# Row sums of a gathered expert layer: both dot products of a pair first, its weights and sums in the same place

## The chip, the cores and the metric

The kernel runs on one core of one Trainium2 chip. The metric is device time of one launch in microseconds (us). The engines are TensorE (PE in the rows, PEld for its weight loads), VectorE (DVE), ScalarE (ACT), GpSimd (POOL) and SyncE (SP); 16 DMA engines move data.

## The reference

A two-block model on 256 tokens of width 1024, all in float32. The part that the change touches is the expert layer of the first block (`peer_ffn`). It runs three times: on the context tokens in layer 0, on the x tokens in layer 0, on the x tokens in layer 1.

```python
def block(args):            # one block of 128 tokens
    hk, ek, gk = args       # tokens [128, 1024], chosen experts [128, 128], gates [128, 128]
    act = jax.nn.gelu(jnp.einsum('ted,td->te', u[ek], hk), approximate=False)
    return jnp.einsum('te,ted->td', gk * act, v[ek])
```

Each token chooses 128 of 16384 experts (8 heads, 16 each, from sums of scores). For each chosen expert a vector u is dotted with the token, the result goes through gelu, is multiplied by the gate and weighs a vector v; the 128 weighted v are summed. Everything else (modulation, a gated recurrence, convolutions, attention, a Fourier convolution, two MLPs) surrounds this.

## The kernel before, in words

The 128 tokens of a tile lie on the 128 partitions. A "row" below is one choice n of all 128 tokens: one indirect DMA from GpSimd (line 2652) gathers 128 pieces of 8 KB, the u and the v of the expert that each token chose, 1 MB in all, into one of `SLOTS` = 6 slots of the buffer `uv`. There are 3 x 2 x 128 = 768 rows, in the order of the list `SELS`, which has seven segments (`SEGS`, line 368): 128 rows of the context tile 0, 32 of context tile 1, 128 + 128 of x in layer 0 (segments 2 and 3, "the x stretch"), the remaining 96 of context tile 1, and 128 + 128 of x in layer 1.

What is done with row j:

- `dot(j)` on VectorE (line 2351): multiply the u half by the token tile (`hA` or `hB`) and add up into a column of `dots`. It shows as CUSTOM_DVE_ANT_0 followed by a small DVE_READ_ACCUMULATOR2_ANT.
- gelu on ScalarE (line 1616), one instruction for both rows of a pair, `dots` to `coef`.
- `weigh(j)` on VectorE: for a row that `on_pe(j)` names, a 128x128 diagonal matrix with coef times gate, written over the head of the slot (line 2361, TENSOR_SCALAR); for any other, coef times gate in one column (line 2363).
- the row sum: for a row on PE two matmuls of the diagonal with the v half, 512 columns each, added up in two PSUM banks (line 1137; each shows as two matmul records because of float32); otherwise one SCALAR_TENSOR_TENSOR on VectorE into `acc` (line 2375; the first of a segment is line 2372). After the last row of a segment `flush` adds both sums to the tokens.

The gather of row j waits until row j - 6 is summed (lines 2640 to 2644), in order of j. A row's slot is therefore taken from the gather's issue until its sum.

`weave` (line 571) sets the order on each engine. It goes over pairs of rows g = 0 to 255 (first weave, ahead of the last layer's mixer) and 256 to 383 (second weave). At each g it issues `segment(g)` and then those pieces of other streams that are due at g by hand-written numbers: projections, recurrence, the choice of experts, modulations, filters. Each engine has its own `segment` and its own pieces of the same numbers, so the instruction order on each engine is fixed. VectorE's `segment(g)` (line 2402) issues: dot of row 2g, weights of the pair g - 1, the VectorE sum of row 2g - 2 if it has one, dot of row 2g + 1, the VectorE sum of row 2g - 1 if it has one. TensorE's `segment(g)` (line 1141) issues the matmuls of the rows of pair g - 1. ScalarE's (line 1611) issues the gelu of pair g.

`on_pe` (line 378): in the x stretch three rows of four are summed on PE (j % 4 != 0), elsewhere every odd row, and in the last 64 rows none.

The weights of all other work come through a ring of two slots of 2 MB, loaded by SyncE's queue as TensorE frees them.

Of the kernel before, what the change touches and what calls it, by code (L numbers as in the profile page):

```python
# [16 lines left out]
ACT = mybir.ActivationFunctionType  # L17
# [54 lines left out]
def program(nc, A, out):  # L72
# [14 lines left out]
    with ctx:  # L87
# [98 lines left out]
        dot_done = sem("dot_done")  # L186
        gelu_done = sem("gelu_done")
# [185 lines left out]
        SEG_END = list(itertools.accumulate(hi - lo for _, _, lo, hi in SEGS))  # L373
# [3 lines left out]

        def on_pe(j):
            w, t, n, seg = SELS[j]
            if seg in (2, 3):  # L380
                return j % 4 != 0
            return j % 2 == 1 and (seg < 6 or n < NSEL // 2)

        pe_upto = list(itertools.accumulate((on_pe(j) for j in range(len(SELS))), initial=0))
# [88 lines left out]
        dots = a.take(4)  # L473
        coef = a.take(4)
# [881 lines left out]
        def _(act):  # L1356
# [254 lines left out]
            def segment(g, first, last):  # L1611

                if g < last:
                    c = slice((g % 2) * 2, (g % 2 + 1) * 2)
                    act.wait_ge(dot_done, 2 * (g + 1))
                    act.activation(coef[:, c], dots[:, c], ACT.Gelu).then_inc(gelu_done, 1)  # L1616

            def kv_pieces():
                for c, dst in enumerate((kcN[:, :, 0:CW], kcN[:, :, CW:D], vN[:, 0:NT, 0:CW], vN[:, 0:NT, CW:D])):
# [162 lines left out]
            for c in range(6):  # L1782
                chunk_there(L_hin, c)
                e = L_hin.e0 + c
                for b in range(4):
                    j = 4 * c + b
# [18 lines left out]
        def _(dve):  # L1805
# [548 lines left out]
            def weigh(j):  # L2354

                p, t, n, seg = SELS[j]
                c = coef[:, column(j):column(j) + 1]
                gate = gates[:, p % 2, t, n:n + 1]
                dve.wait_ge(gelu_done, j // 2 + 1)
                if on_pe(j):  # L2360
                    dve.tensor_scalar(uv[:, j % SLOTS, 0:P], ident[:, :], c, gate, ALU.mult, ALU.mult).then_inc(diag_ready, 1)  # L2361
                else:
                    dve.tensor_tensor(c, c, gate, ALU.mult).then_inc(coef_ready, 1)
# [37 lines left out]

            def segment(g, first, last):

                done = (2 * g - 2, 2 * g - 1) if g > first else ()
                for s in range(2):
                    if g < last:
                        dot(2 * g + s)
                    if s == 0:
                        for j in done:
                            weigh(j)  # L2410
                    if done and not on_pe(done[s]):
                        add_row(done[s])
                if done and 2 * g in SEG_END:
                    flush(SEG_END.index(2 * g))

            def early_mods():
                for c in range(10, 12):
# [334 lines left out]
```

## Time and profile before

| | |
|---|---|
| median of 3 runs | 4079.06 us (4070.0 to 4091.91) |
| the profiled execution | 4078.86 us, span 4077.1 us |
| mean granted TensorE clock | 0.845 of full |
| PE busy | 2923.2 us (72%) |
| DVE busy | 2702.6 us (66%) |
| ACT busy | 669.4 us (16%) |
| POOL busy | 935.1 us (23%) |
| DMA, gathers (queue q0) | 812.33 MB, 51.6% of 16 engines' span |
| DMA, weights and rest (queue q1) | 336.37 MB, 22.8% |

The first row's dot starts at 302.6 us and the last row's at 3186.9 us; between about 2196 and 2344 us the gathers pause for the last layer's mixer. Busy time is not a limit by itself: a stretch ends when its last wait ends. In the rows, "idle before <-releaser" names what ended an engine's idle time.

### The profile page before, as it was taken

How to read it: one execution, taken by the hardware profiler on the slowest of the kernel's cores; microseconds unless marked ns; L12 is line 12 of the kernel's file. 1: busy time of each engine (PE TensorE's matmuls, PEld its weight loads, DVE VectorE, ACT ScalarE, POOL GpSimd, SP SyncE). 2: the span in 40 equal slices, each digit the busy share in tenths (PEclk: the TensorE clock that was granted, in tenths of full speed). 3: DMA queues.
4: the chain of work that ended last, by engine and by line, in shares of the span. 5: the costliest groups of instructions: out<-in, count | busy, mean ns of one | idle time of the engine just before them, and what ended most of it. 6: DMA issues, size and time to landing. Idle time of an engine off the chain costs nothing.

```text
span 4077.1 us, 31583 instructions
## 1 busy us (share of the span) xinstructions
PE 2923.2 (72%) x10786; PEld 1692.8 (42%) x10786; DVE 2702.6 (66%) x5411; ACT 669.4 (16%) x1113; POOL 935.1 (23%) x794
## 2 busy tenths in 40 slices
PE   7988698757888765567976676674570475978598
PEld 2956376324322122224743443111130353967396
DVE  2657968786767678466687577678878754445454
ACT  1311101000000001101002110000000242523053
POOL 0002223333323233233231033233344100000000
PEclk9999799778999887788987878886685697988799
DMA  6359899899999987988996399999899522544144
GB/s 247 123 181 371 301 350 361 330 365 343 368 393 400 368 323 283 345 325 324 356 376 227 124 347 359 384 387 348 334 391 369 203 89 68 186 173 157 57 163 147
DMA packets 277096, 1156.42 MB, mean 284 GB/s; under 512 B 19128, under 2 KB 19769, under 8 KB 178201
## 3 DMA queue, kind: packets, MB, share of 16 engines
q0 software_dynamic: 112768, 812.33, 51.6%
q1 hardware_dynamic: 162584, 336.37, 22.8%
q10 hardware_dynamic: 1600, 5.96, 0.4%
q8 instruction: 71, 1.16, 0.1%
q14 instruction: 73, 0.59, 0.0%
HBM read 1150.46 MB, written 4.13 MB: 283 GB/s over the span
## 4 chain that ended last, share of the span: by engine, by line
PE 40%; DMA 27%; DVE 23%; issue 8%; ACT 1%; POOL 0%; SPq 0%; POOLq 0%; DVEq 0%; PEldq 0%
DMA arena<-in_peer_uv,arena 17%; PE ps L1137 7%; DMA ring<-in_w_mod 7%; PE ps L747 5%; PE ps L749 5%; PE ps L748 5%; PE ps L866 4%; DVE arena L2351 4%; PE ps L1054 3%; DVE arena L2375 3%; PE ps L977 2%; PE ps L732 1%; PE ps L852 1%; DVE w_lo L1927 1%; DVE arena L2361 1%
## 5 line engine op out<-in xcount | busy, mean ns | idle before, releaser
L1137 PE MATMUL ps<-arena 128*128 128x512 f32 x1664 | 1017.2, 752 | 610.1 <-DVE arena L2361 609.8
L2652 POOL DMA_INDIRECT arena<-in_peer_uv,arena x768 | 921.2, 1200 | 2253.1 <-PE ps L1137 846.9
L1137 PEld LDWEIGHTS ps<-arena 128*128 128x128 f32 x1664 | 359.0, 232 | 1196.4 <-DVE arena L2361 801.1
L2351 DVE CUSTOM_DVE_ANT_0 arena<-arena,hA 128x1024 f32<-128x1024 f32 x512 | 624.9, 1223 | 294.2 <-DMA arena<-in_peer_uv,arena 289.3
L2351 DVE CUSTOM_DVE_ANT_0 arena<-arena,hB 128x1024 f32<-128x1024 f32 x256 | 312.8, 1222 | 265.8 <-DMA arena<-in_peer_uv,arena 264.5
L1616 ACT ACTIVATE arena<-arena 128x2 f32<-128x2 f32 x384 | 78.2, 204 | 2384.9 <-DVE arena L2351 2384.3
L2375 DVE SCALAR_TENSOR_TENSOR arena<-arena 128x1024 f32<-128x1024 f32 x345 | 441.0, 1278 | 0.1
L1927 DVE TENSOR_TENSOR w_lo<-ring,w_hi 128x1024 fp32r<-128x1024 f32 x220 | 264.2, 1223 | 161.5 <-ACT w_hi L1396 154.2
L866 PE MATMUL ps<-ring,condS 128*2 128x512 f32 x576 | 284.6, 641 | 77.2 <-DMA ring<-in_w_mod 77.2
L747 PE MATMUL ps<-hT_hi,w_hi 128*128 128x256 f32 x992 | 287.5, 290 | 25.4 <-DVE hT_lo L1935 24.8
L749 PE MATMUL ps<-hT_hi,w_lo 128*128 128x256 f32 x992 | 284.5, 287 | 0.0
L748 PE MATMUL ps<-hT_lo,w_hi 128*128 128x256 f32 x992 | 283.2, 286 | 0.0
L1396 ACT ACTIVATE w_hi<-ring 128x1024 fp32r<-128x1024 f32 x220 | 231.3, 1060 | 239.5 <-DMA ring<-in_w_mlp_out 90.3
L747 PEld LDWEIGHTS ps<-hT_hi,w_hi 128*128 128x128 f32 x992 | 193.2, 195 | 27.7 <-issue 26.8
L1054 PE MATMUL ps<-hT,ring 128*128 128x256 f32 x896 | 201.1, 380 | 1.6 <-ACT hT L1426 1.6
L798 PE MATMUL ps<-ident,hA 128*128 128x128 f32 x128 | 25.5, 376 | 239.5 <-DVE hA L1977 198.5
L748 PEld LDWEIGHTS ps<-hT_lo,w_hi 128*128 128x128 f32 x992 | 193.1, 195 | 0.0
L749 PEld LDWEIGHTS ps<-hT_hi,w_lo 128*128 128x128 f32 x992 | 192.3, 194 | 0.0
L1054 PEld LDWEIGHTS ps<-hT,ring 128*128 128x128 f32 x896 | 170.9, 191 | 44.2 <-issue 21.1
L866 PEld LDWEIGHTS ps<-ring,condS 128*2 128x2 f32 x576 | 45.2, 88 | 307.2 <-issue 217.0
L1101 PE MATMUL ps<-hT,ring 128*128 128x256 f32 x640 | 146.6, 384 | 0.0
L1101 PEld LDWEIGHTS ps<-hT,ring 128*128 128x128 f32 x640 | 124.4, 195 | 33.2 <-issue 17.9
(314 smaller groups left out, 3440.6 us busy)
## 6 DMA issues: line engine op xcount, KB each, us to landing
ring<-in_w_mod SPq DMA_DIRECT2D x48, 2048.0 KB, 19.9
ring<-in_w_in SPq DMA_DIRECT2D x16, 2048.0 KB, 15.3
ring<-in_w_mlp_in SPq DMA_DIRECT2D x64, 512.0 KB, 6.1
ring<-in_w_mlp_out SPq DMA_DIRECT2D x64, 512.0 KB, 5.7
ring<-in_peer_wq SPq DMA_DIRECT2D x12, 2048.0 KB, 16.3
ring<-in_w_in SPq DMA_DIRECT2D x44, 512.0 KB, 5.9
vec<-mods SPq DMA_DIRECT2D x27, 512.0 KB, 8.1
ring<-in_w_out SPq DMA_DIRECT2D x6, 2048.0 KB, 9.0
```

The costliest lines, as they stand in the source:

```text
L747: pe.matmul(out_, stationary[0], moving[0], start=first, stop=False)
L748: pe.matmul(out_, stationary[0], moving[1], start=False, stop=False)
L749: return pe.matmul(out_, stationary[1], moving[0], start=False, stop=last)
L866: mm = pe.matmul(o, condS[:, k, 2 * (l // 2):2 * (l // 2) + 2], ring[:, s, k, :], start=k == 0, stop=k == KT - 1)
L1054: mm = pe.matmul(o, ring[:, s, k, b * P:(b + 1) * P], hT[:, k, :], start=k == 0, stop=k == KT - 1)
L1101: mm = pe.matmul(o, ring[:, s, k, b * P:(b + 1) * P], hT[:, k, :], start=k == 0, stop=k == KT - 1)
L1137: mm = pe.matmul(ps[:, 6 + c, :], uv[:, j % SLOTS, 0:P], uv[:, j % SLOTS, D + c * CW:D + (c + 1) * CW], start=start, stop=stop)
L1396: act.activation(w_hi[:, s, ks, :], ring[:, s, ks, :], ACT.Copy).then_inc(high_done, 1)
L1927: dve.tensor_tensor(w_lo[:, s, ks, :], ring[:, s, ks, :], w_hi[:, s, ks, :].bitcast(F32), ALU.subtract).then_inc(low_done, 1)
L2351: dve.tensor_tensor_reduce(row, row, peer_buf[p][:, t, :], 1.0, 0.0, ALU.mult, ALU.add, dots[:, column(j):column(j) + 1]).then_inc(dot_don ...
L2375: ins = dve.scalar_tensor_tensor(acc, row, c, acc, ALU.mult, ALU.add)
L2652: pool.indirect_dma_start(uv[:, j % SLOTS, :], None, A["peer_uv"], at).then_inc(uv_full[j % SLOTS], 16)
```

## The change

Three edits. VectorE's `segment(g)` issues both dots of pair g, then (after a flush, if a segment of rows ended) the weights of the same pair g and its VectorE sums; before, weights and sums were those of the pair g - 1. ScalarE's gelu is one instruction for each row, with its own wait and its own signal, and `weigh(j)` waits for the gelu of row j alone. `on_pe` no longer makes an exception for the x stretch: there, too, every odd row is on PE.

```diff
--- before.py
+++ after.py
@@ -377,8 +377,6 @@
 
         def on_pe(j):
             w, t, n, seg = SELS[j]
-            if seg in (2, 3):
-                return j % 4 != 0
             return j % 2 == 1 and (seg < 6 or n < NSEL // 2)
 
         pe_upto = list(itertools.accumulate((on_pe(j) for j in range(len(SELS))), initial=0))
@@ -1611,9 +1609,10 @@
             def segment(g, first, last):
 
                 if g < last:
-                    c = slice((g % 2) * 2, (g % 2 + 1) * 2)
-                    act.wait_ge(dot_done, 2 * (g + 1))
-                    act.activation(coef[:, c], dots[:, c], ACT.Gelu).then_inc(gelu_done, 1)
+                    for j in (2 * g, 2 * g + 1):
+                        c = slice(j % 4, j % 4 + 1)
+                        act.wait_ge(dot_done, j + 1)
+                        act.activation(coef[:, c], dots[:, c], ACT.Gelu).then_inc(gelu_done, 1)
 
             def kv_pieces():
                 for c, dst in enumerate((kcN[:, :, 0:CW], kcN[:, :, CW:D], vN[:, 0:NT, 0:CW], vN[:, 0:NT, CW:D])):
@@ -2356,7 +2355,7 @@
                 p, t, n, seg = SELS[j]
                 c = coef[:, column(j):column(j) + 1]
                 gate = gates[:, p % 2, t, n:n + 1]
-                dve.wait_ge(gelu_done, j // 2 + 1)
+                dve.wait_ge(gelu_done, j + 1)
                 if on_pe(j):
                     dve.tensor_scalar(uv[:, j % SLOTS, 0:P], ident[:, :], c, gate, ALU.mult, ALU.mult).then_inc(diag_ready, 1)
                 else:
@@ -2401,17 +2400,16 @@
 
             def segment(g, first, last):
 
-                done = (2 * g - 2, 2 * g - 1) if g > first else ()
-                for s in range(2):
-                    if g < last:
-                        dot(2 * g + s)
-                    if s == 0:
-                        for j in done:
-                            weigh(j)
-                    if done and not on_pe(done[s]):
-                        add_row(done[s])
-                if done and 2 * g in SEG_END:
+                pair = (2 * g, 2 * g + 1) if g < last else ()
+                for j in pair:
+                    dot(j)
+                if g > first and 2 * g in SEG_END:
                     flush(SEG_END.index(2 * g))
+                for j in pair:
+                    weigh(j)
+                for j in pair:
+                    if not on_pe(j):
+                        add_row(j)
 
             def early_mods():
                 for c in range(10, 12):
```

VectorE in the x stretch, a plain place early in segment 2, before. `uv_full3` is the signal that the gather into slot 3 has landed, `gelu_done` and `coef_ready` are the signals of gelu and of a column of coefficients.

```order
L2361 TENSOR_SCALAR arena<-ident,arena 128x128 [waits gelu_done] x2
L2351 ISA arena<-arena,hB 128x1024 [waits uv_full3]
L2351 ISA arena 128x1
L2351 ISA arena<-arena,hB 128x1024 [waits uv_full4]
L2351 ISA arena 128x1
L2363 TENSOR_TENSOR arena<-arena 128x1 [waits gelu_done]
L2361 TENSOR_SCALAR arena<-ident,arena 128x128 [waits gelu_done]
L2375 SCALAR_TENSOR_TENSOR arena<-arena 128x1024 [waits dve_added,coef_ready]
L2351 ISA arena<-arena,hB 128x1024 [waits uv_full5]
L2351 ISA arena 128x1
```

The same place in the changed kernel (line numbers are one lower on VectorE).

```order
L2350 ISA arena<-arena,hB 128x1024 [waits uv_full2]
L2350 ISA arena 128x1
L2350 ISA arena<-arena,hB 128x1024 [waits uv_full3]
L2350 ISA arena 128x1
L2362 TENSOR_TENSOR arena<-arena 128x1 [waits gelu_done]
L2360 TENSOR_SCALAR arena<-ident,arena 128x128 [waits gelu_done]
L2374 SCALAR_TENSOR_TENSOR arena<-arena 128x1024 [waits dve_added,coef_ready]
L2350 ISA arena<-arena,hB 128x1024 [waits uv_full4]
L2350 ISA arena 128x1
L2350 ISA arena<-arena,hB 128x1024 [waits uv_full5]
```

Before, the pair in slots 2 and 3 is weighed and summed (the TENSOR_TENSOR, TENSOR_SCALAR and SCALAR_TENSOR_TENSOR) behind the dot of slot 4, that is, behind a wait for a gather of the next pair; now it stands right behind its own two dots. Each pair has one diagonal and one VectorE sum now, where pairs with two diagonals (the first row shown of before) and pairs with one of each took turns.

VectorE where a piece of other work is due (the choice of experts, which begins with MAX), before.

```order
L2351 ISA arena<-arena,hB 128x1024 [waits uv_full0]
L2351 ISA arena 128x1
L2363 TENSOR_TENSOR arena<-arena 128x1 [waits gelu_done]
L2361 TENSOR_SCALAR arena<-ident,arena 128x128 [waits gelu_done]
L2375 SCALAR_TENSOR_TENSOR arena<-arena 128x1024 [waits dve_added,coef_ready]
L2351 ISA arena<-arena,hB 128x1024 [waits uv_full1]
L2351 ISA arena 128x1
L2222 MAX arena<-arena 128x8 [waits score_out]
```

The same place in the changed kernel.

```order
L2350 ISA arena<-arena,hB 128x1024 [waits uv_full0]
L2350 ISA arena 128x1
L2350 ISA arena<-arena,hB 128x1024 [waits uv_full1]
L2350 ISA arena 128x1
L2362 TENSOR_TENSOR arena<-arena 128x1 [waits gelu_done]
L2360 TENSOR_SCALAR arena<-ident,arena 128x128 [waits gelu_done]
L2374 SCALAR_TENSOR_TENSOR arena<-arena 128x1024 [waits dve_added,coef_ready]
L2221 MAX arena<-arena 128x8 [waits score_out]
```

The pair in slots 0 and 1 was dotted but not weighed when the piece began; now it is weighed, and its VectorE sum issued, ahead of the piece.

ScalarE around a softmax exponential of the choice of experts, before.

```order
L1616 ACTIVATE arena<-arena 128x2 [waits dot_done] x4
L1599 ACT_TABLE_LOAD
L1599 ACTIVATE arena<-arena 128x32 [waits gate_sub]
L1616 ACT_TABLE_LOAD
L1616 ACTIVATE arena<-arena 128x2 [waits dot_done] x5
```

The same place in the changed kernel.

```order
L1615 ACTIVATE arena<-arena 128x1 [waits dot_done] x8
L1597 ACT_TABLE_LOAD
L1597 ACTIVATE arena<-arena 128x32 [waits gate_sub]
L1615 ACT_TABLE_LOAD
L1615 ACTIVATE arena<-arena 128x1 [waits dot_done] x10
```

Each gelu of two columns is two of one; the table loads keep their places and wait for nothing.

## Rows read from the trace of the kernel before

**Rows 1.** Windows, the seven stretches of rows; start:end, length, engines busy, PEclk, DMA, GB/s.

```profile
302.00:810.00 508.00, 407.68 (x1500) 262.05 (x1501) 394.97 (x845) 65.56 (x124) 151.69 (x129) 0.88 0.90 342
810.00:909.00 99.00, 58.46 (x134) 26.61 (x132) 81.58 (x182) 7.93 (x22) 37.22 (x31) 0.76 0.93 365
909.00:1398.00 489.00, 398.76 (x957) 141.17 (x956) 325.06 (x826) 32.66 (x88) 152.72 (x129) 0.92 0.97 378
1398.00:1860.00 462.00, 285.66 (x486) 104.35 (x486) 309.60 (x732) 41.39 (x93) 148.38 (x128) 0.80 0.85 319
1860.00:2196.00 336.00, 263.42 (x962) 166.44 (x963) 253.38 (x453) 34.62 (x73) 108.36 (x93) 0.87 0.92 353
2344.00:2803.00 459.00, 317.90 (x764) 125.11 (x762) 336.39 (x793) 36.43 (x93) 159.16 (x127) 0.80 0.94 370
2803.00:3190.00 387.00, 162.32 (x293) 62.74 (x292) 327.54 (x629) 30.29 (x86) 153.94 (x126) 0.69 0.93 356
sum 2740.00, PE 1894.21 PEld 888.47 DVE 2028.52 ACT 248.89 POOL 911.49; mean PE 270.60 PEld 126.92 DVE 289.79 ACT 35.56 POOL 130.21
```

**Rows 2.** Waits, 302 to 3190 us: who waited for whom, us, times, longest.

```profile
ACT arena L1616 <- DVE arena L2351: 2384.3, 377, 15.8
POOL arena L2652 <- PE ps L1137: 846.9, 284, 16.1
...
POOL arena L2652 <- DVE arena L2375: 734.0, 259, 9.3
...
DVE arena L2351 <- DMA arena<-in_peer_uv,arena: 553.7, 358, 12.1
```

**Rows 3.** Source view of the gather, line 2652, last line.

```profile
DMA to landing us min/median/max: 5.3/8.3/19.2
```

**Rows 4.** Timeline of VectorE around 1000 us; start, duration, instruction, idle before.

```profile
998.28 1.22 DVE L2351 CUSTOM_DVE_ANT_0 arena<-arena,hB 128x1024 f32<-128x1024 f32 x1 [1.29 <-DMA arena<-in_peer_uv,arena]
...
999.78 1.27 DVE L2375 SCALAR_TENSOR_TENSOR arena<-arena 128x1024 f32<-128x1024 f32 x1
1000.99 1.23 DVE L2351 CUSTOM_DVE_ANT_0 arena<-arena,hB 128x1024 f32<-128x1024 f32 x1
...
1007.48 1.23 DVE L2351 CUSTOM_DVE_ANT_0 arena<-arena,hB 128x1024 f32<-128x1024 f32 x1 [5.26 <-DMA arena<-in_peer_uv,arena]
...
1008.63 0.60 DVE L2361 TENSOR_SCALAR arena<-ident,arena 128x128 f32<-128x128 f32 x2
```

**Rows 5.** Timeline of GpSimd in the same place.

```profile
1003.33 0.94 POOL L2652 DMA_INDIRECT arena<-in_peer_uv,arena  x1 [0.30 <-issue]
1013.29 0.94 POOL L2652 DMA_INDIRECT arena<-in_peer_uv,arena  x1 [9.02 <-issue]
```

**Rows 6.** Windows of 100 us, same columns as rows 1.

```profile
400.00:500.00 100.00, 61.15 (x164) 28.36 (x163) 96.27 (x261) 16.72 (x30) 25.70 (x23) 0.76 0.82 304
...
1100.00:1200.00 100.00, 85.55 (x179) 21.41 (x178) 62.01 (x153) 5.44 (x16) 31.62 (x26) 0.93 1.00 398
...
1500.00:1600.00 100.00, 54.93 (x84) 20.71 (x84) 82.73 (x256) 8.24 (x19) 27.43 (x26) 0.77 0.81 299
```

**Rows 7.** Timeline of all engines, 303 to 330 us.

```profile
318.13 0.20 ACT L1616 ACTIVATE arena<-arena 128x2 f32<-128x2 f32 x1
318.37 0.16 DVE L2363 TENSOR_TENSOR arena<-arena 128x1 f32<-128x1 f32 x1 [9.27 <-ACT arena L1616]
...
320.51 0.09 DVE L2351 DVE_READ_ACCUMULATOR2_ANT arena<- 128x1 f32 x1
...
320.63 0.20 ACT L1616 ACTIVATE arena<-arena 128x2 f32<-128x2 f32 x1 [2.29 <-DVE arena L2351]
```

**Rows 8.** Groups of ScalarE by line, 302 to 3190 us.

```profile
L1616 ACT ACT_TABLE_LOAD x39 | 50.0, 1283 | 8.3 <-DVE mod_io L1952 7.6
```

**Rows 9.** Timeline of TensorE, 1734 to 1745 us.

```profile
1735.85 5.28 PE L1137 MATMUL ps<-arena 128*128 128x512 f32 x8 [3.85 <-DVE arena L2361]
1742.26 1.98 PE L1137 MATMUL ps<-arena 128*128 128x512 f32 x4 [1.12 <-DVE arena L2361]
```

## The prediction

> **What bounds the kernel now.** I read the windows by stretch first, then the waits, then the timeline of one place. The seven stretches in which rows are gathered last 2740 us of the 4077.1 us span; nothing outside them is touched. In none of them is one engine full: VectorE is busy 2028.5 us, PE 1894.2 us, and the DMA engines 0.85 to 0.97 [rows 1]. Length times rate gives what each stretch moves: 173.7, 36.1, 184.8, 147.4, 118.6, 169.8 and 137.8 MB, 968 MB in all, a mean of 353 GB/s. A stretch of 100 us in which the DMA engines never rest moves 398 GB/s; one of those without moves 299 [rows 6]. So the stretches lie 11% under the best transfer rate, and the question is what keeps gathers from going out.
>
> The waits say it. GpSimd waits 846.9 us for PE and 734.0 us for VectorE to free a slot; VectorE waits 553.7 us, in 358 of 768 dots, for a gather to land [rows 2]. A row takes 2740 / 768 = 3.57 us, so a slot comes round every 6 x 3.57 = 21.4 us, of which the transfer is 8.3 us in the median [rows 3]. The rest, 13 us, is the wait for the row's turn, its dot, and the time until it is summed. The timeline shows the last part: one pair's dots begin at 998.28 and 1000.99; VectorE then has nothing to do for 5.26 us, until the next pair's first row lands; only behind that row's dot, at 1008.63, come the diagonals of the first pair [rows 4]. GpSimd sends nothing between 1003.33 and 1013.29, 9.02 us of it idle, since the next slot in order belongs to that pair [rows 5]. A finished pair is held by a gather that it needn't wait for.
>
> **Weights and sums of the same pair.** In this place the diagonals could have begun at about 1002.5 instead of 1008.63, 6 us earlier. Everywhere a pair is freed ahead of the next dot, and ahead of any piece of other work that is due between the pairs. On average I expect the hold to fall by about one row's period and a dot, 3.57 + 1.22 = 4.8 us of the 21.4, more where pieces lie between. If transfers stayed at 8.3 us the cycle could shrink by that, to 2.8 us a row. They won't stay: at 398 GB/s a row of 1.049 MB alone needs 2.63 us, and weights come on top. So the latency bound goes nearly everywhere, and what is late next is the DMA engines, with VectorE close behind. Between them no stretch reaches either limit, as the pieces of other work alternate. I count no gain from PE's idle time (it too waited for diagonals).
>
> **What it costs VectorE.** The second row's gelu has nothing in front of it now. From the trace: the accumulator read ends at 320.60, gelu starts at 320.63 and lasts 0.20 us, and VectorE goes on 0.04 us after a gelu (318.33 to 318.37) [rows 7]. That is 0.27 us in which VectorE only multiplies one column, for each of 384 pairs: 104 us, bounds 0 (where VectorE waits for a gather anyway, in 358 of 768 dots) and 104. I take it in full in VectorE's sum for each stretch and let the other limits hide what they hide. The doubled gelu adds 384 x 0.20 = 78 us on ScalarE, which is busy 249 of 2740 us [rows 1] and waited for dots in 377 of 384 gelus [rows 2]: nothing. The 39 table loads of 1.28 us ahead of gelus [rows 8] wait for nothing, stand where they stood, and have a dot of 1.2 us over them: 0 here, at most 39 x (1.28 + 0.20) = 58 us. Behind the waiting VectorE instruction stand that pair's sum and the next dots; GpSimd waits for the sum, 0.27 us later than it could be, yet earlier than before.
>
> **Every other row in the x stretch.** 64 of 256 rows move from PE to VectorE. Each adds a sum, 1.21 us from start to next start (999.78 to 1000.99), and drops a diagonal, 0.30 us of the 0.60 for two [rows 4]; the column product adds under 0.1. That is 1.0 us each, 64 us on VectorE, 32 in each of the two stretches. PE loses 64 row sums of 1.98 us at the high clock or 2.64 at the low one (5.28 for two) [rows 9], 127 to 169 us. Where pairs had two PE rows the slots came free 5.28 us after the diagonals; now one does after 1.98 to 2.64 and the other after VectorE's 1.28. VectorE in these stretches has 325.1 + 32 + 17 = 374 us in 489, and 309.6 + 32 + 17 = 359 in 462: it holds them, though at 1500 us it is busy 83% already [rows 6]. Bounds for this edit alone: +64 us if VectorE set the end everywhere there, -40 us if PE's release did; near 0 taken, as neither does.
>
> The granted clock bears on this: in the second x stretch it is 0.80 with PE busy 286 of 462 us, in the last stretch 0.69 with 162 of 387 [rows 1], so less work on PE goes with more time at 1.2 GHz. The Trainium skill (TensorE: Matmul & The Clock Gate, Part 1) says the same as a rule: the default is the throttled clock and activity releases it. By it the rows left on PE would get slower, against the change. Worked from rows: 64 PE rows in the second x stretch, all at 2.64 instead of 1.98, are 42 us of PE time. PE would then still be busy under 260 of 462 (286, less 32 rows of 1.98, plus 42) us, so I put nothing in the sum for it; it is a part of the slow case below.
>
> **The sum.** For each stretch the DMA floor is its MB at 398 GB/s: 436, 91, 464, 370, 298, 427 and 346 us, 2432 in all, 308 us under now. VectorE's own sum with the new costs is 412, 86, 374, 359, 266, 353 and 345 us. How much of the gap to the floor is taken? The stretches that do best now keep 0.93 to 0.97 of the DMA engines; the first stretch has a part where VectorE is busy 96% and nothing can be won [rows 6]; in the last one both limits lie within a few us, and VectorE at 345 of 387 leaves little. I take 14 of 72 us in the first, 2 of 8, 13 of 25, 37 of 92 (the emptiest, 319 GB/s, goes to 347), 8 of 38, 10 of 32 and 6 of 41: 90 us. That brings the mean to 968 MB in 2650 us, 365 GB/s, what the second stretch does today, and VectorE to 83% (2195 us). The profiled execution took 4078.86 us, 1.8 over its span and 0.2 under the median of 4079.06, so the sum serves for both: 4079 - 90 = 3989 us.
>
> **Rivals.** *Bandwidth is the bound already.* If gathers merely queue in the DMA engines instead of on GpSimd, landing times rise as the holds fall, and VectorE keeps its 553.7 us of waits. For it: stretches at 0.97 and a window at 1.00. Against it: 0.85 in the second x stretch, and 398 GB/s measured. Time: 4079 within 20 us, so 4059 to 4099. The Trainium skill (DMA: Bandwidth & Descriptors, Where 436 GB/s comes from) puts the HBM side at some 358 GB/s for a core and calls it the limit. By that rule 968 MB need 2704 us and at most 36 us could be won, 4043; the windows at 398 [rows 6] speak against it here.
>
> *VectorE's new waits decide (slower).* VectorE waited for no gather in 410 of 768 dots; there the 0.27 us of a pair counts in full: 410 / 768 x 104 = 56 us. Of the 64 us of added sums about half count likewise, 32. If at the same time the early release brings nothing, because the DMA engines or the slower clock on PE hold the slots as long, the time is 4079 + 88 = 4167, and with a gain of a third of mine still 4137. It decides once VectorE is busy over about 0.9 of a stretch; today that is so only around 450 us and in the last stretch (0.85).
>
> *The floor is nearly reached.* Two thirds of the 308 us: 4079 - 205 = 3874. For it: the best window runs at the floor with the long holds. Against: VectorE would have to be busy 0.87 over 2535 us with no piece of work in its way.
>
> **Chances.** Forecast (15 to 165 us won outside the next case's band) 0.66, the floor 0.07, bandwidth 0.15, slower 0.12. A difference of 0.5%, 20 us, is about what a measurement can tell from none. Faster is the first two, 0.73; same 0.15; slower 0.12. The range takes 1 in 10 off each side: 3900 to 4100.
>
> **What would show it.** Right: GpSimd's waits for PE and VectorE fall by some hundreds of us; VectorE's wait for gathers falls under 450 us though the DMA share rises to 0.93 or so; a new wait of the diagonal for gelu appears, near 384 x 0.2 us; the second x stretch gets under 440 us; the diagonals number 352. Wrong: a median landing time of 11 us or more at the same rate (bandwidth), or VectorE over 0.9 busy in most stretches with the time no shorter (slower), or ScalarE found busy or waiting for TensorE when a dot is done, which would make the 0.27 us several times that.

## The result and the profile after

The changed kernel takes 4038.05 us in the median of 4 runs, the kernel before 4083.39 in its 4: ratio 0.989, interval 0.9857 to 0.9923. It is 45 us faster, where 90 were forecast. Faster was right, the size was twice too large. (The profiled executions, from which all rows come, differ by 36 us.)

The page of the changed kernel: its span, and the busy time of each engine.

```profile
span 4041.2 us, 31585 instructions
...
PE 2819.5 (70%) x10530; PEld 1637.4 (41%) x10530; DVE 2787.6 (69%) x5475; ACT 745.7 (18%) x1497; POOL 936.7 (23%) x794
```

VectorE does 85 us more and PE 104 us less than before. The windows of the changed kernel by the same seven stretches of rows, at their new places (columns as in [rows 1]):

```profile
302.00:796.00 494.00, 396.69 (x1508) 259.07 (x1509) 400.14 (x848) 77.63 (x188) 141.77 (x129) 0.91 0.89 350
796.00:896.00 100.00, 57.78 (x127) 25.60 (x126) 82.27 (x182) 11.18 (x38) 37.92 (x32) 0.74 0.93 371
896.00:1406.00 510.00, 354.07 (x833) 119.65 (x832) 361.10 (x858) 45.60 (x152) 147.73 (x129) 0.85 0.91 359
1406.00:1843.00 437.00, 247.92 (x359) 77.67 (x358) 344.23 (x764) 54.00 (x157) 153.69 (x127) 0.69 0.88 342
1843.00:2165.00 322.00, 262.01 (x964) 167.35 (x963) 257.13 (x456) 44.19 (x122) 109.97 (x92) 0.86 0.93 366
2309.00:2782.00 473.00, 313.62 (x765) 124.72 (x766) 341.86 (x796) 49.26 (x157) 150.62 (x129) 0.80 0.92 363
2782.00:3152.00 370.00, 161.70 (x292) 62.31 (x290) 330.32 (x628) 43.24 (x150) 171.63 (x124) 0.67 0.94 368
sum 2706.00, PE 1793.79 PEld 836.38 DVE 2117.04 ACT 325.10 POOL 913.33; mean PE 256.26 PEld 119.48 DVE 302.43 ACT 46.44 POOL 130.48
```

Set against [rows 1], what each stretch gave, by forecast and by trace:

| rows | before, us | after, us | forecast saving | measured saving |
|---|---|---|---|---|
| 0 to 127 | 508 | 494 | 14 | 14 |
| 128 to 159 | 99 | 100 | 2 | -1 |
| 160 to 287 | 489 | 510 | 13 | -21 |
| 288 to 415 | 462 | 437 | 37 | 25 |
| 416 to 511 | 336 | 322 | 8 | 14 |
| 512 to 639 | 459 | 473 | 10 | -14 |
| 640 to 767 | 387 | 370 | 6 | 17 |
| sum | 2740 | 2706 | 90 | 34 |

Five stretches together gave 69 us, 67 forecast. Two got longer, by 35 where 23 less was forecast, and they are the ones in which the modulation's weights (`w_mod`) load, in chunks of 2 MB. Before, the first of them ran its DMA engines at 0.97 of the time and 378 GB/s; now at 0.91 and 359. The transfers are the same; the DMA engines rest more.

The waits of the changed kernel, 302 to 3152 us (who waited for whom, us, times, longest):

```profile
POOL arena L2650 <- PE ps L1135: 867.8, 271, 18.7
...
POOL arena L2650 <- DVE arena L2374: 699.5, 225, 21.4
...
DVE arena L2350 <- DMA arena<-in_peer_uv,arena: 314.0, 214, 6.9
...
PE ps L864 <- DMA ring<-in_w_mod: 194.7, 18, 15.7
...
DVE arena L2360 <- ACT arena L1615: 66.5, 334, 0.2
...
DVE arena L2362 <- ACT arena L1615: 38.0, 39, 11.8
```

VectorE's wait for gathers fell from 553.7 to 314.0 us, as it should. But GpSimd waits for PE and for VectorE nearly as long as before [rows 2], and a wait stands out that the prediction never named: PE's for a chunk of `w_mod`. In the kernel before it was this:

```profile
PE ps L866 <- DMA ring<-in_w_mod: 77.2, 13, 14.0
```

The gathers land hardly later than before [rows 3]:

```profile
DMA to landing us min/median/max: 5.3/8.7/19.0
```

Most of the loss lies in rows 208 to 287, the first stretch of rows beside which modulation chunks load (322 us before, 354 now). The windows, the PE waits for chunks, and issue to landing of chunks and gathers, first before (1076 to 1398 us), then in the changed kernel (1052 to 1406 us; its window stands with the run with four slots below):

```profile
1076.00:1398.00 322.00, 272.00 (x569) 68.27 (x568) 206.68 (x532) 16.53 (x49) 98.46 (x81) 0.93 1.00 397
PE ps L866 <- DMA ring<-in_w_mod: 37.1, 7, 9.2
ring<-in_w_mod SPq DMA_DIRECT2D x21, 2048.0 KB, 21.0
arena<-in_peer_uv,arena POOLq DMA_INDIRECT x81, 9.5
```

```profile
PE ps L864 <- DMA ring<-in_w_mod: 110.7, 11, 15.1
ring<-in_w_mod SPq DMA_DIRECT2D x21, 2048.0 KB, 21.5
arena<-in_peer_uv,arena POOLq DMA_INDIRECT x82, 10.0
```

A chunk lands as late as it did before; what is new is that PE stands before it three times as long.

What happens in such a place, from five views of the changed kernel. TensorE (timeline):

```profile
1329.45 1.98 PE L1135 MATMUL ps<-arena 128*128 128x512 f32 x4
1346.49 5.35 PE L864 MATMUL ps<-ring,condS 128*2 128x512 f32 x8 [15.05 <-DMA ring<-in_w_mod]
1351.77 1.98 PE L1135 MATMUL ps<-arena 128*128 128x512 f32 x4
```

SyncE, which issues the chunks, and GpSimd, which issues the gathers:

```profile
1318.84 0.38 SPq L599 DMA_DIRECT2D ring<-in_w_mod  x1
...
1329.70 0.39 SPq L599 DMA_DIRECT2D ring<-in_w_mod  x1
...
1357.47 0.38 SPq L599 DMA_DIRECT2D ring<-in_w_mod  x1
```

```profile
1334.42 1.41 POOL L2650 DMA_INDIRECT arena<-in_peer_uv,arena  x1 [0.30 <-issue]
1354.56 0.94 POOL L2650 DMA_INDIRECT arena<-in_peer_uv,arena  x1 [18.73 <-PE ps L1135]
```

The source view of the chunks' issues (line 599), 1200 to 1420 us:

```profile
DMA to landing us min/median/max: 18.8/21.7/27.6
```

Windows of the same place, whose last two columns are the DMA engines' share and GB/s:

```profile
1329.00:1344.00 15.00, 2.44 (x6) 0.68 (x4) 9.57 (x16) 0.81 (x4) 3.36 (x3) 0.75 1.02 422
1344.00:1350.00 6.00, 3.51 (x5) 0.59 (x6) 1.92 (x5) 0.20 (x1) 0.00 (x0) 0.50 0.83 310
1350.00:1356.00 6.00, 6.00 (x15) 1.36 (x13) 0.00 (x0) 0.00 (x0) 1.13 (x2) 1.00 0.02 6
```

PE's ring has two chunks of 2 MB. The one that PE waits for is issued at 1318.84, as soon as its place is free, and is there at 1346.4, after 27.6 us, the longest of the row above; the next is issued at 1329.70. Both together at 398 GB/s would be 10.5 us. While gathers are in flight the engines run full (422 GB/s), mostly for them: the DMA records, summed by queue over 3 us each, give the gathers some 0.33 MB/us and the chunks 0.09. When the last gather has landed the chunks get the rest. PE stood before it for 15.05 us, with the matmuls of a finished pair behind in its queue (1351.77); so GpSimd could send nothing for 18.73 us, and from 1350 to 1356 the DMA engines move 6 GB/s. Gathers, then chunks, then nothing: the two streams take turns.

How much of the time is the "nothing" can be counted from the trace, as the time in which no record of 512 bytes or more is under way on any DMA engine, and the gathers in flight by the issue and the landing of each:

| rows 208 to 287 | before | after |
|---|---|---|
| length, us | 322 | 354 |
| no DMA record under way, us | 2.3 | 32.3 |
| gathers in flight, mean | 2.3 | 2.2 |
| share of the time with none in flight | 0.02 | 0.15 |
| share of the time with four or more | 0.07 | 0.16 |

The stretch grew by 32 us and the dead time by 30. In rows 576 to 623, the other such stretch, they grew by 18 and 12 (3.2 to 15.7). So nearly the whole loss is time in which the DMA engines have nothing to do.

### The profile page after: what moved, and what is told of

Read it like the earlier page. It is cut to its first block, busy times and chain, and to the rows that moved or that the text cites. A ratio compares the mean times of both kernels' runs of the same rounds, so it can differ in the third digit from the quotient of the medians.

```text
span 4041.2 us, 31585 instructions
## 1 busy us (share of the span) xinstructions
PE 2819.5 (70%) x10530; PEld 1637.4 (41%) x10530; DVE 2787.6 (69%) x5475; ACT 745.7 (18%) x1497; POOL 936.7 (23%) x794
## 3 DMA queue, kind: packets, MB, share of 16 engines
q1 hardware_dynamic: 162584, 336.37, 22.9%
## 4 chain that ended last, share of the span: by engine, by line
PE 41%; DVE 28%; DMA 25%; issue 3%; ACT 2%; SPq 1%; POOL 0%; DVEq 0%; POOLq 0%; ACTq 0%; PEldq 0%
DMA ring<-in_w_mod 11%; DMA arena<-in_peer_uv,arena 9%; DVE arena L2350 8%; PE ps L1135 6%; DVE arena L2374 5%; PE ps L745 5%; PE ps L747 4%; PE ps L746 4%; PE ps L864 4%; PE ps L1052 4%; PE ps L975 2%; PE ps L730 2%; PE ps L850 1%; DMA vec<-mods 1%; DVE w_lo L1926 1%
## 5 line engine op out<-in xcount | busy, mean ns | idle before, releaser
L2650 POOL DMA_INDIRECT arena<-in_peer_uv,arena x768 | 922.9, 1202 | 2209.9 <-PE ps L1135 867.8
L1135 PE MATMUL ps<-arena 128*128 128x512 f32 x1408 | 895.5, 771 | 518.1 <-DVE arena L2360 503.5
L2350 DVE CUSTOM_DVE_ANT_0 arena<-arena,hA 128x1024 f32<-128x1024 f32 x512 | 614.7, 1222 | 204.0 <-DMA arena<-in_peer_uv,arena 198.7
L1135 PEld LDWEIGHTS ps<-arena 128*128 128x128 f32 x1408 | 300.7, 232 | 1034.5 <-DVE arena L2360 713.1
L1615 ACT ACTIVATE arena<-arena 128x1 f32<-128x1 f32 x768 | 155.0, 203 | 2270.8 <-DVE arena L2350 2269.6
L2374 DVE SCALAR_TENSOR_TENSOR arena<-arena 128x1024 f32<-128x1024 f32 x409 | 523.0, 1279 | 3.8 <-DVE arena L2362 0.3
L745 PEld LDWEIGHTS ps<-hT_hi,w_hi 128*128 128x128 f32 x992 | 192.2, 194 | 28.6 <-issue 27.6
L2360 DVE TENSOR_SCALAR arena<-ident,arena 128x128 f32<-128x128 f32 x352 | 141.3, 401 | 67.2 <-ACT arena L1615 66.5
L1052 PEld LDWEIGHTS ps<-hT,ring 128*128 128x128 f32 x896 | 170.2, 190 | 42.7 <-issue 20.9
## 6 DMA issues: line engine op xcount, KB each, us to landing
ring<-in_w_mod SPq DMA_DIRECT2D x48, 2048.0 KB, 20.8
```

Source lines behind the costliest of these rows:

```text
L745: pe.matmul(out_, stationary[0], moving[0], start=first, stop=False)
L1052: mm = pe.matmul(o, ring[:, s, k, b * P:(b + 1) * P], hT[:, k, :], start=k == 0, stop=k == KT - 1)
L1135: mm = pe.matmul(ps[:, 6 + c, :], uv[:, j % SLOTS, 0:P], uv[:, j % SLOTS, D + c * CW:D + (c + 1) * CW], start=start, stop=stop)
L2350: dve.tensor_tensor_reduce(row, row, peer_buf[p][:, t, :], 1.0, 0.0, ALU.mult, ALU.add, dots[:, column(j):column(j) + 1]).then_inc(dot_don ...
L2374: ins = dve.scalar_tensor_tensor(acc, row, c, acc, ALU.mult, ALU.add)
L2650: pool.indirect_dma_start(uv[:, j % SLOTS, :], None, A["peer_uv"], at).then_inc(uv_full[j % SLOTS], 16)
```

## Experiments

Theory A, as it stood before the runs, has three parts. The early release puts up to six gathers in flight. A gather's packets are of 8 KB, those of a chunk of `w_mod` of 2 KB, and an engine shares itself by packets, so the chunk starves. PE waits for it with finished rows behind, and the slots stay shut. The first part doesn't hold: by the table above the changed kernel has as many gathers in flight as the kernel before, 2.2 in the mean, never six in these rows, and its chunks land no later (21.5 against 21.0 us). The chunk starved before, too. The other two parts are what the runs bear on.

The share can be read from the trace. Over each us in which both queues move data, together over 0.38 MB, the DMA records of rows 208 to 287 give in the median:

| runs of `w_mod` | kernel | gathers, MB/us | chunks, MB/us |
|---|---|---|---|
| 1 KB | changed, run below | 0.37 | 0.05 |
| 2 KB | before | 0.34 | 0.09 |
| 2 KB | changed | 0.33 | 0.09 |
| 16 KB | changed, run below | 0.14 | 0.28 |

These are close to 8 to 1, 4 to 1 and 1 to 2, the ratios of a gather's 8 KB to the length of the run. The Trainium skill (DMA: Bandwidth & Descriptors, Queues, rings and completion order) says that an engine goes round its queues packet by packet. The trace agrees, if one run of a piece or of a chunk is what takes a turn. (By the same section a packet holds several descriptors; equal numbers of runs in a packet on both queues would give these ratios too.)

Rivals: B, VectorE's added sums cost the time; C, the chunk is issued late. Ratios below are to the kernel before, timed beside each run. "Modulation stretches" below are rows 208 to 287 and 576 to 623, from first dot to first dot: 322 + 188 us before, 354 + 206 in the changed kernel.

**The order and the split gelu without the share.**

```diff
         def on_pe(j):
             w, t, n, seg = SELS[j]
+            if seg in (2, 3):
+                return j % 4 != 0
```

> The change with three of four rows still on PE in the x stretch (the order and the split gelu alone). Theory A (early release lets six gathers stand in flight, they take the DMA engines from the modulation's weight chunks, and PE, with its rows queued behind the chunk's wait, stops): the two modulation stretches (rows 208 to 303 and 576 to 623) stay as slow as in the changed kernel, PE's wait for w_mod near 195 us, total within 15 us of 4038. Rival B (the extra sums on VectorE slowed the first modulation stretch): PE's wait for w_mod falls back towards 77 us in the first of the two, total 4038 - 30 or better. My sum put this edit's own effect near zero, bounds -40 to +64.

Measured 3998.26 us, ratio 0.9809 (0.9778 to 0.984). Neither theory had expected it whole: the edit of `on_pe` (from here on "the share": three of four rows on PE, or every other) costs the changed kernel 40 us, and without it the change brings 86, almost the forecast. The modulation stretches take 320 + 208 us, so the first is cured and the second, where this kernel is the changed one, is not. PE's wait for the chunks:

```profile
PE ps L866 <- DMA ring<-in_w_mod: 109.0, 15, 15.8
```

and the windows of about its first modulation stretch, with the DMA engines full again:

```profile
1050.00:1370.00 320.00, 277.38 (x572) 69.18 (x572) 211.00 (x526) 25.73 (x92) 98.50 (x82) 0.91 0.99 396
```

A alone said that the first would stay slow and the total within 15 us of 4038: both wrong. B said that the wait would fall back in the first of the two and the total to 4008 or less: both came. The wait fell by 86 of the 118 us that it had grown, in the first stretch from 110.7 to 41.2 us, where it had been 37.1. So the next runs had to say by which road the share works.

**The share alone.**

```diff
-            if seg in (2, 3):
-                return j % 4 != 0
```

on the kernel before.

> The kernel before with every other row on PE in the x stretch, order and gelu as before. Theory A: the slots are still held by the next pair's gather, so no starved chunk; time 4083 within 20 us. Rival B: slower by 15 to 40 us, most of it between rows 208 and 303. If the share alone makes it faster by over 20 us, part of the measured 45 us is its.

Measured 4077.61 us, ratio 0.9983 (0.9958 to 1.0008): no difference, where B had 15 to 40 us slower. Within it rows 208 to 287 grew from 322 to 340 us, 12 of the 18 as dead time of the DMA engines, and rows 288 to 415 shrank from 462 to 438. PE's wait for chunks rose here too:

```profile
PE ps L864 <- DMA ring<-in_w_mod: 139.7, 17, 14.5
```

A had expected no starved chunk here. PE has 32 us less to do in these rows (240 of 340 us busy, 272 of 322 before) and, as I read it, reaches the next chunk sooner and stands before it longer; so this wait by itself does not measure what a chunk costs.

**w_mod in one run a partition.**

```diff
-            L_mod[l] = linear(chunked(A["w_mod4"][l]), 12)
+            L_mod[l] = linear(whole(A["w_mod4"][l]), 12)
...
+    r["w_mod4"] = w.reshape(4, KT, P, 12, CW).transpose(0, 3, 2, 1, 4)
```

> The changed kernel with w_mod laid out so that a chunk is one run of 16 KB on each partition instead of eight of 2 KB; nothing else moves. Theory A, with the DMA engines sharing by packets (a gather's are 8 KB, a chunk's 2 KB; in the trace a chunk got 0.09 MB/us beside gathers at 0.34): a chunk now gets half or more, PE's wait for w_mod falls from 195 to under 80 us, and the time falls by 40 to 60 us, to 3980 to 4000. Rival (the chunk is late because its issue on SyncE waits for the stored modulation and for PE, not because of the transfer): the wait stays over 150 us and the time within 10 us of 4038.

Measured 3947.29 us, ratio 0.9669 (0.9635 to 0.9702): 91 us under the changed kernel, more than A expected. C is out as the main cause: the order of issues is the same, and the wait is gone, as is the dead time (3.0 us in rows 208 to 287). A chunk's time from issue to landing, from the DMA view of the changed kernel and of this one:

```profile
ring<-in_w_mod SPq DMA_DIRECT2D x48, 2048.0 KB, 20.8
```

```profile
ring<-in_w_mod SPq DMA_DIRECT2D x48, 2048.0 KB, 11.3
```

PE's wait for chunks in the weaves, and the window of the first modulation stretch, with the DMA engines at 409 GB/s, above the 398 that I had taken for their limit (the second has 397). Here gathers do pile up, 3.6 in flight in the mean and up to six, and the chunks land in half the time all the same:

```profile
PE ps L869 <- DMA ring<-in_w_mod: 5.9, 3, 2.4
```

```profile
1055.00:1369.00 314.00, 252.39 (x502) 57.71 (x502) 228.92 (x553) 24.62 (x89) 100.26 (x83) 0.91 0.98 409
```

**The same layout on the kernel before.**

> The kernel before with the same layout of w_mod. Theory A: before, at most four gathers stood against a chunk and the DMA engines ran at 1.00 of their time in this stretch, so there is little to win: 5 to 20 us. The difference to the changed kernel with this layout is then near the 90 us that the sum gave. Rival: it gains as much as the changed kernel does (40 us or more), and then the layout is good by itself and says nothing of the change.

Measured 4073.41 us, ratio 0.9964 (0.9939 to 0.9988): 11 us. So the layout is worth 91 us with the change and 11 without it, though a chunk lands in 11.4 us here against 19.9 in the kernel before, much the same gain. Read the other way, the change is worth 126 us once chunks don't starve, above the 90 forecast.

**Four slots instead of six where chunks load.**

```diff
-                k = j - SLOTS
+                k = j - (4 if 210 <= j < 304 or 578 <= j < 630 else SLOTS)
```

> The changed kernel with gathers 210 to 303 and 578 to 629 each waiting for row j - 4 instead of j - 6, so that at most four stand in flight while modulation chunks load; all else the same. Theory A (six gathers of 8 KB packets starve a chunk of 2 KB packets, and PE's rows stand behind the chunk): the two modulation stretches get shorter than in the changed kernel, 354 + 206 us for rows 208 to 287 and 576 to 623 together falling by 20 to 50, total 3990 to 4020, though gathers are held back. Rival (fewer gathers in flight can only cost in a stretch that moves bytes): the stretches grow, total over 4040.

Measured 3989.84 us, ratio 0.9789 (0.9759 to 0.9819). Holding gathers back made the kernel 48 us faster. It is the sharpest test: no byte, packet or instruction is another, only a gather's issue waits for an earlier or later row. It does not put fewer gathers in flight, though: their mean number stays 2.2. It spreads them evenly: none in flight for 0.01 of the time instead of 0.15, four or more for 0.04 instead of 0.16, and the dead time of rows 208 to 287 falls from 32.3 to 4.3 us. PE's wait for chunks in the weaves and issue to landing in rows 208 to 287, then the windows of this run over the two modulation stretches, and those of the changed kernel:

```profile
PE ps L864 <- DMA ring<-in_w_mod: 6.0, 3, 4.9
ring<-in_w_mod SPq DMA_DIRECT2D x21, 2048.0 KB, 15.5
arena<-in_peer_uv,arena POOLq DMA_INDIRECT x82, 8.7
```

```profile
1055.00:1385.00 330.00, 254.60 (x504) 57.94 (x502) 229.98 (x553) 24.60 (x89) 91.27 (x82) 0.91 0.97 385
2476.00:2668.00 192.00, 140.46 (x265) 33.85 (x264) 134.61 (x314) 15.33 (x54) 56.18 (x49) 0.86 0.97 384
```

```profile
1052.00:1406.00 354.00, 241.92 (x493) 53.70 (x492) 230.40 (x552) 24.61 (x89) 90.40 (x82) 0.85 0.89 352
2520.00:2726.00 206.00, 132.31 (x260) 30.82 (x259) 134.68 (x314) 15.32 (x54) 52.52 (x48) 0.81 0.90 355
```

**Three of four rows on PE, with the layout.**

> The new order and split gelu with three of four rows on PE in the x stretch, and w_mod in runs of 16 KB. It tells what the share edit costs where no chunk starves. Theory A: the 40 us between the changed kernel and the one without the share edit were starved chunks alone, so this is within 12 us of the changed kernel with this layout (3947). Rival B (the 64 sums on VectorE cost by themselves): it is faster than 3947 by 20 us or more.

Measured 3940.9 us, ratio 0.9662 (0.9627 to 0.9696), 6 us under the run with every other row, intervals overlapping. Where no chunk starves the share costs next to nothing; so of its 40 us in the changed kernel most, about 33 by the medians, go through the chunks. B, the sums by themselves, is out as the main cause. By what step the share brings the turns about was not measured. The trace shows only where they are: with the new order and every other row on PE no DMA record is under way for 32.3 us of rows 208 to 287 and 15.7 of rows 576 to 623; with three of four rows on PE for 4.6 of the first. The modulation stretches of this run are the fullest of all:

```profile
1050.00:1353.00 303.00, 271.30 (x580) 71.54 (x579) 211.21 (x532) 24.61 (x89) 93.95 (x82) 0.97 1.01 423
2447.00:2623.00 176.00, 132.77 (x257) 31.60 (x256) 134.11 (x314) 15.33 (x54) 61.19 (x48) 0.89 0.99 402
```

**The even row's sum first.**

```diff
                 for j in pair:
                     weigh(j)
-                for j in pair:
                     if not on_pe(j):
                         add_row(j)
```

> The changed kernel with the even row weighed and summed before the odd row is weighed, so that the odd row's gelu passes under a sum of 1.28 us instead of leaving VectorE idle; the odd row's diagonal comes about 1 us later. If the 104.5 us that VectorE now waits for gelu stand on the path in full: 60 to 90 us faster. If, as in my sum, they are mostly hidden by the DMA engines: within 15 us. If the odd row's release is what counts: slower by 10 to 30.

Measured 4029.44 us, ratio 0.9872 (0.9836 to 0.9908), 9 us under the changed kernel, intervals overlapping. The diagonal's wait for gelu is gone from the list (66.5 us before this edit), and the time hardly moves: the wait is hidden almost whole, as the sum had it.

**One gelu for each row, alone.**

```diff
-                    act.wait_ge(dot_done, 2 * (g + 1))
-                    act.activation(coef[:, c], dots[:, c], ACT.Gelu).then_inc(gelu_done, 1)
+                    for j in (2 * g, 2 * g + 1):
+                        c = slice(j % 4, j % 4 + 1)
+                        act.wait_ge(dot_done, j + 1)
+                        act.activation(coef[:, c], dots[:, c], ACT.Gelu).then_inc(gelu_done, 1)
...
-                dve.wait_ge(gelu_done, j // 2 + 1)
+                dve.wait_ge(gelu_done, j + 1)
```

> The kernel before with one gelu for each row, nothing else. ScalarE waits for dots in nearly all gelus and is busy a tenth of the rows' time, so 768 instead of 384 gelus should cost nothing: within 12 us of 4085. The other reading, that ScalarE's doubled work delays evictions: slower by 20 us or more.

Measured 4080.33 us, ratio 1.0003 (0.9988 to 1.0019): nothing.

**w_mod in runs of 1 KB.**

```diff
-            L_mod[l] = linear(chunked(A["w_mod4"][l]), 12)
+            L_mod[l] = linear(halved(A["w_mod4"][l]), 12)
...
+    w = w.reshape(4, KT, P, 12, 2, CW // 2).transpose(0, 1, 4, 2, 3, 5)
```

> The changed kernel with a chunk of w_mod in sixteen runs of 1 KB on each partition instead of eight of 2 KB: the opposite of the layout in runs of 16 KB. Theory A (the DMA engines share by packets): beside gathers a chunk gets still less, its time to landing rises over 25 us, PE's wait for w_mod over 250 us, and the total rises by 30 to 90 us over 4038. Rival (the size of the runs mattered only by the transfer's own speed, alone): at most 10 us over 4038.

Measured 4059.84 us, ratio 0.9931 (0.9899 to 0.9963), 22 us over the changed kernel. The intervals of the two ratios overlap a little, but the fastest of its runs (4053.21) is slower than the slowest of the changed kernel (4043.01). The sign is A's, the size under its 30 to 90, and so is the wait under its 250; the trace of this run has no landings, so the 25 us can't be checked:

```profile
PE ps L872 <- DMA ring<-in_w_mod: 222.4, 18, 17.3
```

A share strictly by packets would halve the chunk's part beside gathers, and by the table above it did, from 0.09 to 0.05 MB/us. PE's wait goes the same way for 1, 2 and 16 KB (222, 195 and 6 us) but not in proportion. One reason can be read from the DMA records of rows 208 to 287: in 68 us, against 38 in the changed kernel, chunks move at over 0.2 MB/us with hardly any gather beside them. What the chunk loses beside gathers it makes up alone.

**TensorE's sums in the place of their own pair.**

```diff
-                if g > first:
-                    for j in (2 * g - 2, 2 * g - 1):
+                if g < last:
+                    for j in (2 * g, 2 * g + 1):
```

> The changed kernel with TensorE's row sums also in the place of their own pair, ahead of the pieces of other work of that pair. Part of theory A is that finished rows stand in PE's queue behind its wait for a chunk, so that no gather goes out while the chunk lands and the DMA engines run dry after it. With the sums ahead of that wait the slots come free: GpSimd's waits for PE (868 us) fall under 600 and the total falls by 20 to 60 us. Against: more gathers in flight starve the chunks more, and PE must wait for a diagonal before it starts the pieces; then 4038 or slower.

Measured 4064.46 us, ratio 0.9952 (0.9932 to 0.9972): a miss, 26 us slower than the changed kernel. GpSimd's wait for PE did fall, though not under the 600 expected (its wait for VectorE rose, from 699.5 to 873.7):

```profile
POOL arena L2650 <- PE ps L1135: 663.4, 245, 19.0
...
PE ps L864 <- DMA ring<-in_w_mod: 158.9, 18, 15.3
```

The modulation stretches got shorter, 339 + 192 us, but rows 48 to 95 went from 179 to 212 and rows 432 to 511 from 418 to 437. In rows 48 to 95 PE was busy 172 of the 179 us in the changed kernel; now it waits 16 us there for diagonals, so the work that is queued behind them comes later.

**The same, only where chunks load.**

```diff
+                def own(g):
+                    return 104 <= g < 152 or 288 <= g < 314
...
```

> The changed kernel with TensorE's row sums in the place of their own pair for the pairs 104 to 151 and 288 to 313 alone, where modulation chunks load. In the run with this order everywhere the two modulation stretches took 339 + 192 us instead of 354 + 206, but the stretches with projections lost 52. If finished rows behind PE's wait for a chunk are a part of the cause: 15 to 35 us under 4038, 4003 to 4023, with the projection stretches as in the changed kernel. If only the chunk's share of the DMA engines counts: within 10 us of 4038.

Measured 4000.03 us, ratio 0.9798 (0.9775 to 0.9821), 38 us under the changed kernel, a little more than the 15 to 35 expected. Rows 48 to 95 take 179 us again, the modulation stretches 337 + 197, and the dead time in them falls from 32.3 + 15.7 to 17.5 + 8.6 us. PE's wait for chunks is still there, a fifth shorter, and GpSimd's wait for PE 138 us less:

```profile
POOL arena L2653 <- PE ps L1135: 730.3, 256, 17.9
...
PE ps L864 <- DMA ring<-in_w_mod: 159.7, 18, 14.9
```

A chunk lands as late as in the changed kernel here (20.8 us in the median, on both pages). So two parts of A are shown, each by an edit that leaves the other alone: chunks land late by their share of the DMA engines (the layout), and part of the damage comes from finished rows queued behind PE's wait for them (this run).

**All weights in one run, sum first.** The layout of `whole` for every weight, with the sum-first order.

> A version to beat both: the changed kernel, all weights laid out in one run on each partition (16 KB a chunk, 4 KB a quarter), and the even row's sum ahead of the odd row's diagonal. w_mod alone gave 3947; the other weights load beside gathers in about a third of the rows, and in the MLPs alone: I expect 3900 to 3940. If only the modulation's chunks mattered: 3930 to 3947.

Measured 3950.44 us, ratio 0.9656 (0.9612 to 0.97): as fast as with `w_mod` alone, and a miss against the 3900 to 3940 expected, by 3 us also against the 3947 named for the other case. Nothing shows that other chunks than the modulation's mattered. This one, the layout on the changed kernel and the layout with three of four rows (3940.9) can't be told apart; all beat both kernels by a wide margin.

## Why the prediction was wrong

The direction and the main mechanism held. One step of the sum failed, and with it the term for every other row.

- **The hold of a finished pair.** Right. VectorE's wait for gathers went from 553.7 to 314.0 us, under the 450 named. Where no modulation loads, the stretches gave 69 us of 67 forecast; single ones are off by up to 12.
- **The cost to VectorE.** Right in kind, 0.27 us for 384 pairs, 104 us. The trace has 66.5 + 38.0 = 104.5, and that this meets the forecast to a us is luck: 22.8 of the 38.0 are two long waits, and the kernel before had two such waits of 18.4 us together. The regular ones are 0.2 us each, some 73 us in all. That they would be hidden nearly whole is borne out by the 9 us that the sum-first order brought.
- **The doubled gelu.** Right, 0 (4080.33 against 4079.17).
- **Every other row in the x stretch, "near 0 taken".** Wrong with the new order, where it costs 40 us, inside the bound of 64 but not by the mechanism priced. VectorE held its sums; what they do to the turns of gathers and chunks was not in the sum. The granted clock of the second x stretch fell from 0.80 to 0.69, and the stretch still got 25 us shorter. The trace agrees with the rule of the Trainium skill (TensorE: Matmul & The Clock Gate, Part 1) that less activity goes with the lower clock. It cost nothing that shows: with the layout, rows 288 to 415 take 410 us at a granted clock of 0.71 (every other row on PE) and 416 at 0.81 (three of four).
- **A reading within it.** "2.64 at the low one" is not a row at the low clock: the 5.28 us for two rows [rows 9] begin at the low clock and end at the high one. A row wholly at the low clock (granted 0.51 from 1723 to 1729 us) took 3.78:

```profile
1724.12 3.78 PE L1137 MATMUL ps<-arena 128*128 128x512 f32 x4 [3.92 <-DVE arena L2361]
```

  So 64 such rows would cost 115 us of PE time more than at the high clock, not 42, and the bound on PE, "under 260 of 462", is too low. Nothing in the sum hung on it.
- **The sum: "the DMA engines ... what is late next", 13 of 25 and 10 of 32 us.** This is the step that failed. It took the DMA engines as one limit that a stretch can only approach, so that an earlier release could win or be neutral. It left out that they serve two streams in unequal parts (0.33 to 0.09 MB/us), and that the one that loses stands ahead of finished rows in PE's queue, so that both streams stop while PE waits. The two terms came out at -21 and -14, 58 us from the 23 forecast, against 56 missing in the sum of the stretches (90 less 34). In their place the trace shows 42 us more in which no DMA record is under way, in rows 208 to 287 and 576 to 623. The first term alone would have held without the share: with the new order and three of four rows on PE, rows 160 to 287 take 474 us, 15 under the kernel before, where 13 were forecast. Both would have held with long runs: 468 and 449 us, 21 and 10 under.
- **The sign that failed.** "GpSimd's waits for PE and VectorE fall by some hundreds of us": they did not (846.9 to 867.8 and 734.0 to 699.5), though the dots waited less. It hints that slots are shut for a new reason, but it was set too high: in the run with the layout, 137 us faster than the kernel before, the two waits still come to 500.6 + 911.1 = 1412 us, 169 under the 1581 of before.
- **The rivals.** Bandwidth as the bound already is out for the rows as a whole: landing times rose only from 8.3 to 8.7 us, and the runs with the layout hold up to 423 GB/s. In rows 208 to 287 it stood near: the kernel before ran its DMA engines at 1.00 there, with 397 GB/s. The Trainium skill's 358 GB/s (DMA: Bandwidth & Descriptors, Where 436 GB/s comes from) is no limit here, where a single core runs. VectorE's waits deciding is out too. None of the rivals was the starved chunk, though the trace before held it: PE waited 77.2 us for `w_mod`, and a chunk took 19.9 us to land.
- **What stays open.** Why an order and a share that each leave the first modulation stretch at 320 and 340 us make it 354 together, with as many gathers in flight and chunks landing as late.

## What to carry to other kernels

Before buffers are released sooner, list who else uses the DMA engines then, in what packet sizes, and what is queued behind the wait for them. Two streams with one consumer queue can fall into turns: one lands, the consumer stands before the other, and then neither moves. Three things broke the turns here: longer runs in memory for the stream that loses (91 us), fewer buffers for the other while it loads (48 us), and finished work ahead of the wait, in that place alone (38 us). Count the time in which nothing moves before naming the number of transfers in flight as the cause: here the number was the same.

## What the runs showed of the hardware

- A chunk of 2 MB in runs of 2 KB took 20.8 us to land (the median of 48, most of them beside gathers in runs of 8 KB), and 11.3 us in runs of 16 KB, at the same bytes; the packets on its queue, by the page of the profile, fell from 162584 to 119576.
- With both queues busy, gathers and chunks moved 0.37 and 0.05 MB/us with chunks in runs of 1 KB, 0.33 and 0.09 at 2 KB, 0.14 and 0.28 at 16 KB: near 8, 4 and a half to one.
- Gathers and long runs together moved 423 GB/s over 303 us; with runs of 2 KB the same stretch had 397 in the kernel before.
- Fewer slots gave more bytes: 385 GB/s with four against 352 with six, in the first modulation stretch of the changed kernel, at the same mean number of gathers in flight (2.2) and with 4.3 instead of 32.3 us in which none of the DMA engines works.
- A row's matmuls took 1.98 us at the high clock and 3.78 at the low one.
